# A decoder layer on one core: the mixer in two phases, 13 of its 16 projection pairs by Strassen's products

## The reference, cut to what matters

```
z = h @ w_mix_in
q, k, v, g_lr, og, cu, gates = split(z)          # widths 512, 512, 1024, 16, 1024, 2048, 2048
log_a = log_sigmoid(g_lr @ gla_w_gate_up + gla_b_gate) / 16
o = gla_chunked(q, k, v, log_a)                  # gated linear attention, 4 heads, causal
y_gla = (rms_norm(o, gla_norm_g) * silu(og)) @ gla_w_proj
ua, ub = split(cu);  u = ua * sigmoid(ub)
u = silu(layer_norm(causal_depthwise_conv(u, conv_dw_w, conv_dw_b)))    # 31 taps per channel
y_conv = u @ conv_w_proj
gate_a, gate_b = split(sigmoid(gates))
return (gate_a * y_gla + gate_b * y_conv) @ w_mix_out
```

## Time and profile before

| | |
|---|---|
| median of 3 runs | 2311.94 us (2310.87 to 2312.35) |
| profiled execution, first to last instruction (its span) | 2309.1 us |
| what lies around the span, against the median | 2.8 us (the profiled execution has no time of its own beside its span) |
| PE, DVE, ACT, POOL busy | 2291.4, 1577.5, 844.0, 783.2 us |
| mean granted TensorE clock | 0.999 |
| mixer's first head up to its second score level | to 738.17 us; the same point of the next heads 917.03, 1095.89, 1274.75 |

### The profile page before, as it was taken

One profiled execution on the slowest core, in us unless ns is written; L12 is line 12 of the kernel. 1 busy time (PEld: TensorE's weight loads), 2 busy tenths in 40 slices (PEclk: granted clock), 3 DMA queues, 4 the chain that ended last, 5 costly groups with the idle time before them and its releaser, 6 DMA issues.

```text
span 2309.1 us, 29786 instructions
## 1 busy us (share of the span) xinstructions
PE 2291.4 (99%) x10784; PEld 1904.0 (82%) x10784; DVE 1577.5 (68%) x1988; ACT 844.0 (37%) x1227; POOL 783.2 (34%) x529
## 2 busy tenths in 40 slices
PE   8999999999999999999999999999999999999998
PEld 5888888888878888888888888888888888888887
DVE  8856665677755885785795686742586666667677
ACT  5433333343664234234224232422343333333443
POOL 3454455100432223213313236223565445540002
PEclk9999999999999999999999999999999999999999
DMA  5333333557832022122123135444323333338566
GB/s 157 114 91 114 91 114 91 191 178 225 290 97 73 29 83 74 38 83 83 28 74 101 37 127 201 146 139 144 119 69 91 114 91 116 96 95 266 161 223 232
DMA packets 238963, 281.89 MB, mean 122 GB/s; under 512 B 11408, under 2 KB 164752, under 8 KB 236048
## 3 DMA queue, kind: packets, MB, share of 16 engines
q1 hardware_dynamic: 232336, 267.98, 37.0%
q10 hardware_dynamic: 6528, 12.58, 1.4%
HBM read 208.17 MB, written 72.35 MB: 121 GB/s over the span
## 4 chain that ended last, share of the span: by engine, by line
PE 69%; DVE 1%; ACT 0%; POOL 0%; issue 0%; DMA 0%; POOLq 0%; DVEq 0%; ACTq 0%
PE PU L719 11%; PE PU L721 11%; PE PU L720 11%; PE PU L854 4%; PE PU L852 4%; PE PU L853 4%; PE PU L1003 2%; PE PU L1004 2%; PE PU L1005 2%; PE PG L854 2%; PE PG L852 2%; PE PG L853 2%; PE PG L1097 2%; PE PG L1004 1%; PE PG L1003 1%; PE PG L1005 1%
## 5 line engine op out<-in xcount | busy, mean ns | idle before, releaser
L719 PE MATMUL PU<-XH,w_h 128*128 128x512 f32 x992 | 392.8, 396 | 0.8 <-POOL w_l L2696 0.8
L721 PE MATMUL PU<-XH,w_l 128*128 128x512 f32 x992 | 386.5, 390 | 0.0
L720 PE MATMUL PU<-XL,w_h 128*128 128x512 f32 x992 | 386.1, 389 | 0.0
L2701 POOL TENSOR_TENSOR ws<-pw,ws 128x512 fp32r<-128x512 f32 x168 | 244.0, 1456 | 215.2 <-ACT ws L1374 185.1
L2406 DVE SCALAR_TENSOR_TENSOR PG<-ub,cw,PG 128x512 f32<-128x512 f32 x464 | 307.9, 750 | 0.1
L2696 POOL TENSOR_TENSOR w_l<-w_raw,w_h 128x2048 fp32r<-128x2048 f32 (+1 forms) x39 | 175.4, 4497 | 309.2 <-ACT w_h L1277 309.2
L719 PEld LDWEIGHTS PU<-XH,w_h 128*128 128x128 f32 x992 | 186.3, 188 | 40.0 <-POOL w_l L2696 1.3
L2701 POOL TENSOR_TENSOR ws<-s_sum,ws 128x512 fp32r<-128x512 f32 x122 | 159.8, 1319 | 173.8 <-ACT ws L1374 173.8
L721 PEld LDWEIGHTS PU<-XH,w_l 128*128 128x128 f32 x992 | 186.2, 188 | 39.2
L720 PEld LDWEIGHTS PU<-XL,w_h 128*128 128x128 f32 x992 | 186.4, 188 | 38.4 <-issue 0.5
L2116 DVE TENSOR_TENSOR f_l<-f_raw,f_h 128x1024 fp32r<-128x1024 f32 x110 | 139.4, 1273 | 54.8 <-ACT f_h L1553 54.7
(11 more groups left out here) (426 smaller groups left out, 5347.2 us busy)
## 6 DMA issues: line engine op xcount, KB each, us to landing
pw<-in_ffn_w_in SPq DMA_DIRECT2D x86, 512.0 KB, 5.6
f_raw<-f_d SPq DMA_DIRECT2D x154, 256.0 KB, 3.2
f_raw<-in_ffn_w_out SPq DMA_DIRECT2D x132, 256.0 KB, 4.2
w_raw<-in_w_mix_in SPq DMA_DIRECT2D x50, 512.0 KB, 5.2
f_d<-s_buf SPq DMA_DIRECT2D x22, 1024.0 KB, 5.0
f_d<-hid SPq DMA_DIRECT2D x21, 512.0 KB, 2.6
x_d<-FACC SPq DMA_DIRECT2D x16, 512.0 KB, 3.3
gate_d<-tmp ACTq DMA_DIRECT2D x16, 512.0 KB, 2.8
```

The source lines that it names most:

```text
L719: pe.matmul(dst, hi(k), xh(k), start=(n == 0), stop=False)
L720: pe.matmul(dst, hi(k), xl(k), start=False, stop=False)
L721: last = pe.matmul(dst, lo(k), xh(k), start=False, stop=(n == KT - 1))
L2701: PT(ws[:, i, 1, :, :], form_source(name, par), ws[:, i, 0, :, :], ALU.subtract).then_inc(form_lo, 1)
```

## The change

The mixer's projections are put in two phases, and 13 of the 16 pairs are computed in another way.

**Phase A** begins with the low-rank gate, convolution pair 0 (a block in each of the first two tiles) and pair 1 (a unit), and then takes 13 pairs, C2 to C7 and G0 to G6 in turn. Each is a 2x2 product (weights: two blocks of columns by two halves of k; activations: two halves of k by two halves of the tokens) in Strassen's scheme with 7 products of 12 matmuls. The products are summed in PSUM: P1, P6, P7 and P4 follow one another in one bank, P2 alone and then P5, P3 in another; ACT copies what the bank holds after P1, P6 and P7, and DVE adds the other bank to the copies. The activation forms T1 to T4 are made once, by DVE, with ACT and POOL as before for the parts. The convolution's u goes to HBM (`u_d`) and comes back; its first four channel tiles are convolved in this phase, 1024 tokens to an instruction.

**Phase B** is the four heads, now with three tiles each (QK, v, output gate as one tile of two blocks), and the eighth gate pair. The attention steps of a head stand between them: states, outputs and out_transposes of head h-1 within QK and v of head h, levels 0 to 6 from the end of v to the end of the output gate. The other four channel tiles of the convolution (in 512s) lie between the attention's work on DVE.

Core of the diff (lines left out are marked with dots; the order of each engine is shown as it is called):

```diff
-S_GP = S_HEAD + 8 * HEADS
+PAIRS = (("C", 2), ("G", 0), ("C", 3), ("G", 1), ("G", 2), ("C", 4), ("G", 3), ("C", 5), ("G", 4), ("C", 6),
+         ("G", 5), ("C", 7), ("G", 6))
+MIX_FORM = {"P1": "A11", "P2": "A12", "P6": "S2", "P5": "S1", "P7": "S3", "P4": "A22", "P3": "S4"}
+CONV_P = (6, 5, 3, 3)
+CONV_B = ((14, 4, 6, 24, 0, 0, 14), (6, 3, 5, 18, 4, 4, 10))
...
 # PE, phase A
+            def mix_product(j, name):
...
+                elif name == "P3":
+                    pe.wait_ge(c22_done, C22_0 + j + 1)
+                elif name == "P5":
+                    pe.wait_ge(c11_done, C11_0 + j + 1)
+                else:
+                    pe.wait_ge(m_copy, 3 * j + ("P6", "P7", "P4").index(name) + 1)
+                dst = PU[:, p, 0 if name in ("P1", "P6", "P7", "P4") else 1, :]
+                first, final = name in ("P1", "P2", "P5"), name in ("P2", "P3", "P4")
+                for k in range(4):
+                    pe.matmul(dst, form[:, 0, k, :], hi[:, k, :], start=first and k == 0, stop=False, skip_group_check=True)
+                    pe.matmul(dst, form[:, 0, k, :], lo[:, k, :], start=False, stop=False, skip_group_check=True)
+                    last = pe.matmul(dst, form[:, 1, k, :], hi[:, k, :], start=False, stop=final and k == 3,
+                                     skip_group_check=True)
...
+            for j in range(1, NP):
+                mix_product(j, "P1")
+                mix_product(j - 1, "P4")
+                mix_product(j, "P2")
+                mix_product(j - 1, "P3")
+                mix_product(j, "P6")
+                mix_product(j, "P5")
+                mix_product(j, "P7")
+            mix_product(NP - 1, "P4")
+            logits(0)
+            mix_product(NP - 1, "P3")
 # PE, a head of phase B
+                unit(u, 0, s, 0, 2, between=(lambda: logits(h)) if h else None)
+                before(states, 0)()
+                unit(u, 1, s, 1, 2, between=before(states, 1))
+                before(outputs, 0)()
+                v_unit(u + J_V, s + J_V, 0, before(outputs, 1))
+                before(out_transposes, 0)()
+                v_unit(u + J_V, s + J_V, 1, before(out_transposes, 1), lambda: keys(h))
+                level(h, 0)
+                level(h, 1)
+                unit(u + J_OG, 0, s + J_OG, 0, 2, between=lambda: (level(h, 2), level(h, 3)))
+                level(h, 4)
+                level(h, 5)
+                unit(u + J_OG, 1, s + J_OG, 1, 2, halfway=(None, lambda: level(h, 6)))
+                diagonal(h)
 # ACT, a head of phase B (after the rounding of v's weights and the logits' Abs, Exp, Ln)
+                query_keys(h, 0)
+                exps(h, 0, 3)
+                query_keys(h, 1)
+                ahead(h, J_OG)
+                if h:
+                    head_outputs(h - 1, 0)
+                    head_outputs(h - 1, 1)
...
+                values(h, 1)
+                ahead(h + 1, J_QK)
...
+                exps(h, 4, 6)
+                out_gates(h, 0)
+                exps(h, 6, 8)
+                out_gates(h, 1)
+            def out_gates(h, half):
...
+                A(og[:, :, tok], PU[:, half, :, :], ACT.Copy)
+                A(tmp[:, half, :, :], PU[:, half, :, :], ACT.Sigmoid).then_inc(unit_free[half], 1)
 # DVE, into phase A (t0, t1 and the T forms are 128 x 2048)
+            TT_(t0[:, :, :], quadrant(XH, "B12"), quadrant(XH, "B11"), ALU.subtract).then_inc(t_step, 1)
+            TT_(t1[:, :, :], quadrant(XH, "B22"), quadrant(XH, "B12"), ALU.subtract).then_inc(t_step, 1)
+            rank_lo(1)
...
+            t_lo(1, "T1")
+            TT_(t0[:, :, :], quadrant(XH, "B22"), t0[:, :, :], ALU.subtract).then_inc(t_step, 1)
+            t_lo(2, "T3")
...
+            mix_add(0, "C11")
+            t_lo(4, "T4")
 # DVE, a head of phase B
+                    chain(h - 1, 0, 4)
+                dve.wait_ge(b_done, h + 1)
+                for m in range(3):
+                    minus(m)
+                if h:
+                    chain(h - 1, 4, 7)
+                head_taps(h, 2)
...
+                for m in range(3):
+                    times(h, m)
+                head_taps(h, 3)
...
+                minus(3)
+                times(h, 3)
+                select(h, 0)
+                minus(4)
+                select(h, 1)
+                minus(5)
+                times(h, 4)
+                times(h, 5)
+                select(h, 2)
+                minus(6)
+                select(h, 3)
+                minus(7)
...
+                times(h, 6)
+                times(h, 7)
+                select(h, 4)
+                select(h, 5)
+                head_taps(h, 6)
+                select(h, 6)
+                select(h, 7)
 # POOL, phase A: for pair j + 1 four sums (mix_sum) and seven remainders (mix_rest), and the product u_pair; a head:
+                lo(s + J_V)
+                lo(s + J_OG)
+                if h:
+                    out_scales(h - 1, 0)
+                    out_scales(h - 1, 1)
+                lo(s + 3)
```

More of the change, by code:

```diff
@@ new lines, in tile_done, with raw_free, place, made @@
+def tile_done(s):
+    if s < S_PAIR:
+        return s + 1
+    if s < S_B:
+        return S_PAIR + form_at(s - S_PAIR, "P3") + 1
+    return S_PAIR + 7 * NP + s - S_B + 1
+def raw_free(s):
+    if S_PAIR <= s < S_B:
+        return S_PAIR + form_at(s - S_PAIR, "P4") + 1
+    return tile_done(s)
+def place(s):
+    return s % 2 if s < S_PAIR else (s + 1) % 2
+def made(j, name):
+    return form_at(j, name) + 1
+def sigs(j, name):
+    n = 0
+    for t in range(NP + 1):
+        here = [(t - 1, "C22"), (t - 1, "C21")] if t else []
+        if t < NP and PAIRS[t][0] == "G":
+            here.append((t, "C11"))
+        if t and PAIRS[t - 1][0] == "G":
+            here.append((t - 1, "C12"))
+        if (j, name) in here:
+            return n + here.index((j, name)) + 1
+        n += len(here)
@@ new lines, in outputs @@
+            def outputs(h, half):
+                if half == 0:
+                    pe.wait_ge(qb_ready, h + 1)
+                freed(h, H_O + half)
+                for c in range(4 * half, 4 * half + 4):
+                    dst = GL[:, (c % 4) * DV:(c % 4 + 1) * DV]
+                    pe.matmul(dst, A_sb[:, c, :], v_sb[:, c, :], start=True, stop=False)
+                    last = pe.matmul(dst, qb[:, c * P:(c + 1) * P], S_sb[:, c, :], start=False, stop=True)
+                last.then_inc(g_done, 1)
@@ L1192, in gp @@
+            for h in range(HEADS):
+                head(h)
+            unit(U_G7 // 2, 0, S_G7, 0, 2, between=lambda: states(HEADS - 1, 0))
+            states(HEADS - 1, 1)
+            unit(U_G7 // 2, 1, S_G7, 1, 2, between=lambda: outputs(HEADS - 1, 0))
+            outputs(HEADS - 1, 1)
             def gp(e, half, halfway=None):
-                unit(U_GP // 2 + e, half, S_GP + e, (S_GP + e) % 2, half, 2, None, GP_KS, halfway)
+                unit(U_GP // 2 + e, half, S_GP + e, half, 2, None, GP_KS, halfway)
@@ new lines, in mix_gate @@
+            def mix_gate(j, name):
+                f, half = int(name[1]) - 1, int(name[2]) - 1
+                dst = mixed(j)[:, f, half, :]
+                if name == "C21":
+                    act.wait_ge(m_done, made(j, "P4"))
+                    A(dst, PU[:, j % 2, 0, :], ACT.Sigmoid).then_inc(sig_done, 1)
+                    return
+                done, n = {"C11": (c11_done, C11_0), "C12": (c12_done, C12_0), "C22": (c22_done, C22_0)}[name]
+                act.wait_ge(done, n + j + 1)
+                A(dst, dst, ACT.Sigmoid).then_inc(sig_done, 1)
@@ new lines, in _, with ahead, exps @@
+            for j in range(NP + 1):
+                period(j)
+            def ahead(h, j):
+                t = 3 * h + j
+                if t == 1:
+                    act.wait_ge(m_done, 7 * NP)
+                    hi(S_B + 1, None)
+                else:
+                    hi(S_B + t, U_B + 2 * (t - 1))
+            def exps(h, first, last):
+                for m in range(first, last):
+                    act.wait_ge(d_ready, 8 * h + m + 1)
+                    r = R[:, 1, 0:HALF] if m == 1 else R[:, m % 3, :]
+                    A(r, r, ACT.Exp, scale=1.0 / 16).then_inc(e_ready, 1)
```

1269 lines of the change are left out of this document (746 added, 523 removed).

## The result

| | before | after |
|---|---|---|
| median of 4 runs each | 2312.14 us (2310.87 to 2313.08) | 2342.57 us (2341.87 to 2345.35) |
| span of the profiled execution | 2309.1 us | 2340.4 us |
| mean granted TensorE clock | 0.999 | 0.988 |

The kernel became slower: ratio 1.0137, interval 1.0125 to 1.0149. 2332 was forecast, with 2303 to 2352 as the range. The span grew by 31.3 us where the sum had 20.5.

A forecast was written before the change was run, and what follows sets the result against it. PE's instruction stream was taken as the bound; -35.5 us of matmuls plus waits at the way in and heads summed to +20.5 on the 2309.1 span, 2329.6, and with a 2.8 offset 2332.4 us; range 2303 to 2352.

The forecast's parts named there:

- the clock: Rival, chance 0.12: after some eight PE waits one product each runs at 1.2 GHz, 2.7 us more each, 22 in all: 2354.
- the way in: Start of the pair phase: T forms on DVE alternate with POOL, so early products and taps come late, +15.0 us (2 to 20).
- the layout: Main case, chance 0.50: all waits as summed from the new order of work, with its own range 2318 to 2344.
- What goes: 13 projection pairs take 84 matmuls by Strassen instead of 96: 156 fewer on PE, -35.5 us, held for certain.
- The pair phase: 13 periods of 19.1 us in which DVE, ACT and POOL keep up, so PE waits cost nothing.
- Level five: In each head, Exps on ACT stand behind out_gates(h,0), so PE waits for times(6): +5.9 us, four times, 23.6.
- Outputs: Heads 1 to 3: outputs(h-1,1) waits for ON because POOL does lo(OG) before the root: +2.0 us each.
- Head 0: Levels two and three late by 3.0 and 6.4 us, behind DVE taps and POOL's w_l: +9.4, plus 0.8 at its door.
- The state chain: In the heads, logits, Ln, subtraction, scan and chain end 0.8 us before states(h-1,1) is due: 0 us.
- the tail: After head 3, the eighth gate pair covers states and outputs: 0 us, bounds -2 and +5.

The follow-up runs named there:

- The last kernel: The next head's q and k weight rounding on ACT moved behind the Exps, added to the kernel with T4's rounding behind P6's copy: 2288.18 us, 0.9899 of the kernel before.
- the first experiment: Kernel after, with exps(h,6,8) done together with exps(h,4,6), ahead of out_gates(h,0), in all four heads: 2315.43 us, 1.0016 of the kernel before.
- the sixth experiment: Kernel after, with DVE adding C11 of the first pair before T4's two steps instead of behind them: 2346.1 us, 1.0151 of the kernel before.
- the kernel with the four edits: Kernel after, with Exps before out_gates, root before output gate's weights, thirteen tap halves out of head 0, C11 before T4: 2297.8 us, 0.9942 of the kernel before.
- the second experiment: Kernel after, with 20 matmuls of unused result between levels four and five in each head: 2338.45 us, 1.0117 of the kernel before.
- the third: Kernel after, with Sigmoid before the copy in out_gates so the table loads lie differently: 2339.31 us, 1.0121 of the kernel before.

## Why the prediction was right, and where it was off

The sign, the place and the kind of nearly every wait were right. The time was 10 us short, from two errors of opposite sign: the clock, which stood beside the sum as a rival, was missing from it (17.7), and the way in was too large (by 7.6). That 2342.6 still lies in the layout's own range of 2318 to 2344 is luck of this kind: the forecast with the clock and with the way in as summed would have been 2350.

- *What goes, -35.5.* Right: 156 matmuls fewer (10784 to 10628), and a pair takes 19.04 us, where 96 matmuls at 0.2275 are 21.84; 13 times the difference is 36.4. The last kernel shows the same for the heads: with their waits gone, one is 91.7 us, as counted (91.5).
- *The pair phase, 0.* Right: 19.04 us a pair, PE busy for all of it at clock 1.00. DVE's busy time was 15.2 and POOL's 16.3 in that one, against some 15 and 16.9. All eleven periods from P1 to P1 on PE's timeline are 19.04.
- *Level five, 5.9 four times.* Right to 0.2 (5.7), and shown by the first experiment, which moves nothing but the Exps. The chain was as laid out: copy, load, Sigmoid, load, Exp, product.
- *Outputs, 2.0 three times.* Right (2.1), shown by POOL's order alone.
- *Head 0, 9.4 at levels two and three.* Right (9.0: 2.9 and 6.1), and the cause too. The taps in front set level two: moved away, its 2.9 went. At level three `w_l` sits inside a `minus` (m = 4, where the prediction had 5), 4.99 us on DVE beside 4.63 on POOL:

```profile
1031.25 4.99 DVE L2844 TENSOR_TENSOR R<-b_sb 128x512 f32<-128x512 f32 x1
```

- *The way in, +15.0: the term that was too large.* It measured 7.4. The alternation was right. In the kernel after:

```profile
680.67 2.28 DVE L2705 TENSOR_TENSOR tf<-XH 128x2048 f32<-128x2048 f32 x1
...
691.91 3.38 DVE L2710 TENSOR_TENSOR tf<-tf,XL 128x2048 f32<-128x2048 f32 x1
695.22 3.38 DVE L2712 TENSOR_TENSOR tf<-tf,XL 128x2048 f32<-128x2048 f32 x1
...
728.42 0.69 DVE L2731 TENSOR_TENSOR tmp<-PU,tmp 128x512 f32<-128x512 f32 x1
...
736.52 2.60 DVE L2744 TENSOR_SCALAR PG<-ub,cw,cols 128x1024 f32<-128x1024 f32 x2 [3.42 <-DMA ub<-u_d]
```

```profile
693.11 3.33 POOL L3285 TENSOR_TENSOR w_raw<-w_raw 128x512 f32<-128x512 f32 x1
```

  An operation of 2.28 alone has a pitch of 3.3 beside POOL (691.91 to 695.22), and POOL's of 1.27 takes 3.33. But the layout let errors of a few tenths add up over forty us: the add for C11 came at 728.4, not 732.2, and the first taps at 736.5, not 741. So P5 waited 3.9 instead of 6.2, P6 3.0 instead of 3.9, P1 of the first pair not at all instead of 1.5, and P3 and P5 of the next pair, for which 3.4 were summed, not at all either; 0.5 more came at the third tile.
- *The state chain and the tail, 0 each.* Right: no wait of PE in the list is theirs.
- *The clock, a rival at 0.12: the term that was missing from the sum.* The rival had it at 2.7 for each of eight waits, 22 on top of the layout; it measured 17.7, on top of the layout. The step that failed is the reason given against it: the wait of 5.7 at the start, in a slice with 9 granted, was taken to show that a wait costs no clock. The reading was wrong, not only the case a special one. Behind that wait the matmuls of the kernel before stand 0.85 us apart and later 0.43, with 1.00 in the clock column all the while, and every wait of 5.7 in the heads loses 2.2 to 2.7. The rule from the Trainium skill that the prediction cites (TensorE: Matmul & The Clock Gate, Part 1: an idle engine at 1.2 GHz) was set aside on that one figure; in the trace after it agrees, with 0.50 granted inside each of those waits. By the spacing of the matmuls it agreed in the trace before as well. Filling the waits shows the cause.

By sums, 20.5 became 31.2: -7.6 at the way in, +0.9 before the heads, -0.3 in them, and +17.7 by the clock.

## What to carry to other kernels

When a bound engine's work is cut, list for each of its steps what it waits for in the new order, queue by queue on the other engines: here 35.5 us were saved and 49 lost to waits, and 17.7 more to the clock; 28.8 of those 49 went with the place of one Exp on ACT and one root on POOL. A wait of TensorE like those here, 3.9 to 6.1 us between dense work, costs its length and some 1.6 to 3.2 us of half clock behind it. Read the rate from the spacing of equal matmuls, not from the clock column alone. Moving one instruction earlier only helps if its engine has time: at the way into the pairs three moves handed one wait from DVE (3.9) to ACT (6.0) and on to POOL (6.0).

## What the runs showed of the hardware

- Waits of 3.9 us and more were each followed by half clock, up to some 6 us into the work behind them, with 512-column matmuls 0.427 us apart instead of 0.2275. The 5.7 at the kernel's start was too, by the matmuls' spacing (0.85 and later 0.43), though the granted clock in the record is 1.00 there.
- Shorter waits differ. The 3.05 and the 2.94 of the kernel after had half clock behind them, and so had the 3.26 of the sixth experiment; the 3.07 at T2 in the kernel with the four edits had not. Of the three waits of 2.1 on ON none had it in the kernel after, two in the first and the second experiment, and three in the third. What decides there is open.
- Useless matmuls in such waits made the kernel faster: 19 us of them, 4.1 us less.
- DVE and POOL, each with operations that read SBUF tiles (two inputs on DVE), take turns where both have work: 2.28 becomes 3.38 and 1.27 becomes 3.3, and a 0.69-us subtraction caught by a 4.6-us one takes 5.
